# Two output projections cut into tiles of four contraction tiles by 512 columns, with the head norms moved behind their first tiles

## What is computed

```
mix1 = concat(gated linear attention heads (4 x 128), sliding window heads (8 x 64))   # 256 x 1024
o_gla = rms_norm(o_gla per head, gla_norm_w) * silu(gg)
x = x + gate * (mix1 @ attn_w_out)            # first block; then rms_norm and the first MLP
mix2 = concat(block attention heads (8 x 64), retention heads (4 x 128))               # 256 x 1024
ret = (ret - mean per head) * rsqrt(var per head + 1e-5) * ret_norm * silu(rg)
x = x + mix2 @ w_out_2                        # last block; then rmsnorm and the gated FFN
```

## Time and profile before

| | us |
|---|---|
| Median of 3 runs (1048.24 to 1051.0) | 1048.71 |
| Span of the profiled execution, first to last instruction | 1042.5 |
| TensorE busy | 935.5 (90%) |
| VectorE busy | 684.2 (66%) |
| ScalarE busy | 483.4 (46%) |
| GpSimd busy | 56.2 (5%) |
| HBM read | 194.38 MB, 187 GB/s over the span |
| Mean granted TensorE clock | 0.927 of full speed |

### The profile page before, as it was taken

One profiled execution on the slowest core, in us unless ns is written; L12 is line 12 of the kernel. 1 busy time (PEld: TensorE's weight loads), 2 busy tenths in 40 slices (PEclk: granted clock), 3 DMA queues, 4 the chain that ended last, 5 costly groups with the idle time before them and its releaser, 6 DMA issues.

```text
span 1042.5 us, 17856 instructions
## 1 busy us (share of the span) xinstructions
PE 935.5 (90%) x7128; PEld 893.5 (86%) x7128; DVE 684.2 (66%) x864; ACT 483.4 (46%) x566; POOL 56.2 (5%) x102
## 2 busy tenths in 40 slices
PE   1599987999999999599999996999876999999976
PEld 1398865989999999499999995988776999999976
DVE  5847977767887677665655457455546777666456
ACT  1426543346663325356663335444535565633353
POOL 2101111021111000000000000000000000000000
PEclk9689976979999997889999997999988999999988
DMA  9839764639988876047765554433413555655511
GB/s 327 282 132 313 265 200 141 201 101 320 324 309 298 273 250 222 0 142 228 236 218 164 193 174 137 160 123 124 160 41 106 178 175 187 208 162 176 192 41 41
DMA packets 156457, 196.09 MB, mean 188 GB/s; under 512 B 5325, under 2 KB 143100, under 8 KB 156412
## 3 DMA queue, kind: packets, MB, share of 16 engines
q1 hardware_dynamic: 142588, 145.12, 43.5%
q0 software_dynamic: 13824, 50.34, 13.2%
HBM read 194.38 MB, written 1.06 MB: 187 GB/s over the span
## 4 chain that ended last, share of the span: by engine, by line
PE 75%; DVE 14%; ACT 4%; issue 4%; DMA 1%; SPq 1%; DVEq 0%; ACTq 0%; POOLq 0%
PE G L517 15%; PE G L518 15%; PE G L519 15%; PE A L517 7%; PE A L518 7%; PE A L519 7%; DVE w_lo L949 2%; ACT w_hi L1537 2%; PE A L597 1%; PE A L577 1%; DVE HN L1096 1%; DVE ada_acc L967 1%; PE G L551 1%; PE G L552 1%; PE G L553 1%
## 5 line engine op out<-in xcount | busy, mean ns | idle before, releaser
L949 DVE TENSOR_TENSOR w_lo<-raw,w_hi 128x2048 fp32r<-128x2048 f32 (+1 forms) x135 | 307.1, 2275 | 228.8 <-ACT w_hi L1537 228.7
L517 PE MATMUL G<-h_hi,w_hi 128*128 128x256 f32 x1336 | 392.7, 294 | 44.4 <-DVE h_lo L1078 26.7
L1537 ACT ACTIVATE w_hi<-raw 128x2048 fp32r<-128x2048 f32 (+1 forms) x135 | 256.6, 1901 | 339.0 <-PE G L519 167.2
L518 PE MATMUL G<-h_lo,w_hi 128*128 128x256 f32 x1336 | 387.0, 290 | 0.0
L519 PE MATMUL G<-h_hi,w_lo 128*128 128x256 f32 x1336 | 386.5, 289 | 0.0
L517 PEld LDWEIGHTS G<-h_hi,w_hi 128*128 128x128 f32 x1336 | 265.6, 199 | 52.0 <-issue 38.4
L518 PEld LDWEIGHTS G<-h_lo,w_hi 128*128 128x128 f32 x1336 | 266.2, 199 | 0.5 <-issue 0.5
L519 PEld LDWEIGHTS G<-h_hi,w_lo 128*128 128x128 f32 x1336 | 265.7, 199 | 0.0
L517 PE MATMUL A<-u_hi,w_hi 128*128 128x256 f32 x512 | 143.6, 281 | 0.9 <-DVE X L1058 0.9
L518 PE MATMUL A<-u_lo,w_hi 128*128 128x256 f32 x512 | 143.2, 280 | 0.0
L519 PE MATMUL A<-u_hi,w_lo 128*128 128x256 f32 x512 | 143.2, 280 | 0.0
(11 more groups left out here) (265 smaller groups left out, 1058.6 us busy)
## 6 DMA issues: line engine op xcount, KB each, us to landing
raw<-in_mlp_w_dram SPq DMA_DIRECT2D x64, 1024.0 KB, 5.5
ada_raw<-in_ada_w_dram POOLq DMA_DIRECT2D x90, 512.0 KB, 5.3
raw<-in_w_in_dram SPq DMA_DIRECT2D x14, 1024.0 KB, 5.0
raw<-in_w_up_dram SPq DMA_DIRECT2D x11, 1024.0 KB, 5.3
raw<-in_w_gate_dram SPq DMA_DIRECT2D x11, 1024.0 KB, 5.3
raw<-in_attn_w_in_dram SPq DMA_DIRECT2D x9, 1024.0 KB, 12.2
raw<-in_w_down_dram SPq DMA_DIRECT2D x8, 1024.0 KB, 5.1
raw<-in_attn_w_out_dram SPq DMA_DIRECT2D x4, 1024.0 KB, 5.9
```

The source lines that it names most:

```text
L517: pe.matmul(dst, wh, ah, start=start, stop=False)
L518: pe.matmul(dst, wh, al, start=False, stop=False)
L949: dve.tensor_tensor(w_lo[n % 2][:, 0:k, :], raw[n % RAW][:, 0:k, :], w_hi[n % 2][:, 0:k, :].bitcast(F32), ALU.subtract).then_inc(lo_done, 1)
L1537: act.activation(w_hi[n % 2][:, 0:k, :], raw[n % RAW][:, 0:k, :], ACT.Copy).then_inc(hi_done, 1)
```

## The change

Both projections are cut another way: each of the four 1 MB blocks is now 4 tiles of the contraction by 512 columns. Blocks 0 and 1 are the attention half of the contraction for columns 0 to 511 and 512 to 1023; they open all four G banks and leave them open. Blocks 2 and 3 add the other half in the same banks. `out_block` does 48 matmuls, as a block did. In projection 1, block 0 stands ahead of the sums of squares; in projection 2, block 0 stands between means and variances and block 1 behind the variances. The retention scores of all four heads are made ahead of the last input block, in four banks. ScalarE makes the high half of block 11 (in projection 2: of blocks 93 and 94) ahead of the head roots, VectorE the low half likewise. On VectorE, projection 1's eleven pieces of modulation stood 4, 3, 2, 1, 1 and now stand 2, 2, 7; the seven come after the low halves of the normed activations and ahead of all four `residual_pair`. In projection 2 the gate product is moved behind the squares of the deviations. A residual may start when two of a block's four column tiles are done (`out_half`).

```diff
+OUT_TILES = ((slice(4, 8), slice(0, 4)), (slice(0, 4), slice(4, 8)))
...
+        def half_k(block):
+            return block[:, :, :].rearrange("p (a b) n -> p a (b n)", b=2)
...
-        take_each(*((f"rs{h}", h % 2) for h in range(4)))
-        take_each(("ro0", 2), ("ro1", 3), ("rm0", 0), ("rm1", 1), ("rv0", 2), ("rv1", 3), ("ms6", 2),
+        take_each(*((f"rs{h}", h) for h in range(4)))
+        take_each(("ro0", 0), ("ro1", 1), ("rm0", 2), ("rm1", 3), ("rv0", 0), ("rv1", 1), ("ms6", 2),
...
+            def load_half(n, w, tiles, half):
+                sp.wait_ge(lo_done, n - RAW + 1)
+                sp.dma_start(half_k(raw[n % RAW]), w[:, tiles, half * 2 * COLS:(half + 1) * 2 * COLS]
+                             ).then_inc(raw_full[n % RAW], 16)
...
+            def out_block(layer, j, split):
+                n, half, cut = (N_OUT, N_OUT2)[layer] + j, j // 2, j % 2
+                first = (U_OUT, U_OUT2)[layer] + 2 * cut
+                block_ready(n)
+                hi, lo = half_k(w_hi[n % 2]), half_k(w_lo[n % 2])
+                for m in range(4):
+                    u, cols = first + m // 2, slice(m * P, m * P + P)
+                    if half == 0 and m % 2 == 0:
+                        g_empty(u)
+                    for a in range(4):
+                        if cut == 0 and m == 0 and a % 2 == 0:
+                            pe.wait_ge(h_ready, 4 * SPLIT[split] + 2 * half + a // 2 + 1)
+                        ka = OUT_TILES[layer][half].start + a
+                        last = product(halves(G[u % 4])[:, m % 2, :], hi[:, a, cols], lo[:, a, cols],
+                                       h_hi[:, ka, :], h_lo[:, ka, :], half == 0 and m % 2 == 0 and a == 0,
+                                       half == 1 and a == 3, shared=True)
+                    if half == 1 and m == 1:
+                        last.then_inc(out_half, 1)
+                last.then_inc(block_used, 1)
...
+            out_block(0, 0, "mix0")
             for m in range(2):
                 pe.wait_ge(osq_ready, m + 1)
                 dst = bank_empty(pe, f"gm{m}")
...
-            for j in range(4):
-                feature_block(N_OUT + j, 9 + j, split="mix0" if j == 0 else None,
-                              order=(4, 5, 6, 7, 0, 1, 2, 3))
+            for j in range(1, 4):
+                out_block(0, j, "mix0")
...
-                    retention_scores((0, 1))
-            retention_scores((2, 3))
+                    retention_scores(range(4))
...
+                out_block(1, j, "mix1")
+            for j in (2, 3):
+                out_block(1, j, "mix1")
...
-            ada_next(1, 4)
             for a, p in enumerate((2, 3)):
                 low_pair("mix0", p, MIX[:, 2 * p:2 * p + 2, :], position=a)
+            ada_next(1, 2)
...
-            ada_next(1, 3)
+            ada_next(1, 2)
+            split_lo(N_OUT + 2)
...
-            for j in range(3):
-                split_lo(N_OUT + j + 2)
-                ada_next(1, (2, 1, 1)[j])
-                residual_pair(N_OUT + j, 9 + j, 2 * j, MOD[:, 0, 2 * DT:])
-            residual_pair(N_OUT + 3, 12, 6, MOD[:, 0, 2 * DT:])
+            split_lo(N_OUT + 3)
+            ada_next(1, 7)
+            for j in range(4):
+                residual_pair(N_OUT + 2 + j // 2, U_OUT + j, 2 * j, MOD[:, 0, 2 * DT:],
+                              half=0 if j % 2 else j // 2 + 1)
+                if j == 1:
+                    split_lo(N_OUT + 4)
...
+            split_lo(N_IN2 + 15)
+            split_lo(N_OUT2 + 2)
...
-            for j in range(3):
-                split_lo(N_OUT2 + j + 2)
-                residual_pair(N_OUT2 + j, U_OUT2 + j, 2 * j, None)
-            residual_pair(N_OUT2 + 3, U_OUT2 + 3, 6, None)
+            split_lo(N_OUT2 + 3)
+            for j in range(4):
+                residual_pair(N_OUT2 + 2 + j // 2, U_OUT2 + j, 2 * j, None, half=0 if j % 2 else 3 + j // 2)
+                if j == 1:
+                    split_lo(N_OUT2 + 4)
...
+            split_hi(N_OUT + 2)
             head_roots(("gm0", "gm1"), eps6)
...
             bank_was_read(act, "att_out17")
+            act.wait_ge(block_used, N_IN2 + 14)
             for p in range(2):
                 high_mix(p)
-            for m in range(2):
-                src = bank_full(act, f"ro{m}")
-                bank_read(f"ro{m}", act.activation(GG[:, 2 * m:2 * m + 2, :], halves(src), ACT.Copy))
+                src = bank_full(act, f"ro{p}")
+                bank_read(f"ro{p}", act.activation(GG[:, 2 * p:2 * p + 2, :], halves(src), ACT.Copy))
+            silu_parts(N_IN2 + 13, U_IN2 + 13, RT[:, 2:4, :], RG[:, 2:4, :])
+            split_hi(N_OUT2 + 1)
+            split_hi(N_OUT2 + 2)
             head_roots(("rv0", "rv1"), eps5)
```

More of the change, by code:

```diff
@@ L60 @@
 FDOWN_KT = (8, 8, 6)
-U_POOL, U_UP, U_IN2, U_OUT2, U_FFN, U_PLE, U_PLEG = 29, (13, 33), 49, 63, 67, 89, 93
+U_OUT, U_POOL, U_UP, U_IN2, U_OUT2, U_FFN, U_PLE, U_PLEG = 9, 29, (13, 33), 49, 63, 67, 89, 93
 C_ID, C_ANTI, C_HOT, C_MASK, C_DIST, C_DECAY, C_CNT = 0, 128, 256, 384, 512, 768, 1792
@@ L266, in build @@
         a_free = sems(*(f"a_free{n}" for n in range(4)))
-        down_half, down_free0, down_free1 = sems("down_half", "down_free0", "down_free1")
+        down_half, down_free0, down_free1, out_half = sems("down_half", "down_free0", "down_free1", "out_half")
         dve_step, act_step, pe_step = sems("dve_step", "act_step", "pe_step")
@@ L411, in _ @@
                 for j in range(4):
-                    load(N_OUT + j, w_out1[:, :, j * COLS:(j + 1) * COLS])
+                    load_half(N_OUT + j, w_out1, OUT_TILES[0][j // 2], j % 2)
                 for layer in range(2):
@@ L430, in _ @@
                 for j in range(4):
-                    load(N_OUT2 + j, w_out2[:, :, j * COLS:(j + 1) * COLS])
+                    load_half(N_OUT2 + j, w_out2, OUT_TILES[1][j // 2], j % 2)
                 with sp.Fori(0, 5) as i:
@@ L513, in _, with product @@
             chain = Chain(pe, pe_step)
[L515 to L519, removed]
+            def product(dst, wh, wl, ah, al, start, stop, shared=False):
+                pe.matmul(dst, wh, ah, start=start, stop=False, skip_group_check=shared)
+                pe.matmul(dst, wh, al, start=False, stop=False, skip_group_check=shared)
+                return pe.matmul(dst, wl, ah, start=False, stop=stop, skip_group_check=shared)
             def block_ready(n, i=0):
@@ L537, in feature_tile, with feature_block @@
                 return last
-            def feature_block(n, u, split=None, i=0, order=range(KT)):
+            def feature_block(n, u, split=None, i=0):
                 block_ready(n, i)
@@ L543, in feature_block @@
                     last = feature_tile(n, halves(G[u % 4])[:, m, :], slice(m * P, m * P + P),
-                                        [(k, k) for k in order], h_hi, h_lo, split=split if m == 0 else None)
+                                        [(k, k) for k in range(KT)], h_hi, h_lo, split=split if m == 0 else None)
+                last.then_inc(block_used, 1)
[17 more added lines that the diff above has]
+                        last.then_inc(out_half, 1)
                 last.then_inc(block_used, 1)
@@ L861, in _ @@
                     bank_done(f"ro{m}", last)
-            for name, src in (("rm", GG), ("rv", OSQ)):
+            for j, (name, src) in enumerate((("rm", GG), ("rv", OSQ))):
                 for m in range(2):
@@ L870, in _ @@
                                                       start=True, stop=True))
-            for j in range(4):
-                feature_block(N_OUT2 + j, U_OUT2 + j, split="mix1" if j == 0 else None)
+                out_block(1, j, "mix1")
+            for j in (2, 3):
+                out_block(1, j, "mix1")
             mean_square(6)
@@ L1024, in add_squares, with residual_pair @@
                 dve.wait_ge(ssq_ready, ssq[0])
-            def residual_pair(n, u, t, gate, squares=True):
-                dve.wait_ge(block_used, n + 1)
+            def residual_pair(n, u, t, gate, squares=True, half=0):
+                if half:
+                    dve.wait_ge(out_half, half)
+                else:
+                    dve.wait_ge(block_used, n + 1)
                 src = halves(G[u % 4])
@@ L1403, in _ @@
             for h in range(4):
-                if h == 2:
-                    split_lo(N_IN2 + 15)
                 src = bank_full(dve, f"rs{h}")
@@ L1424, in _ @@
                 dve.tensor_tensor(OSQ[:, 2 * m:2 * m + 2, :], o, o, ALU.mult).then_inc(osq_ready, 1)
+            for m in range(2):
+                u = U_IN2 + 12 + m
+                dve.wait_ge(g_free[u % 4], u // 4 + 1)
+                chain(dve.tensor_tensor(RG[:, 2 * m:2 * m + 2, :], RG[:, 2 * m:2 * m + 2, :],
+                                        RT[:, 2 * m:2 * m + 2, :], ALU.mult))
+            split_lo(N_IN2 + 15)
+            split_lo(N_OUT2 + 2)
             for m in range(2):
@@ L1750, in _ @@
```

(5 more changed lines are left out.)

## The result

Twelve runs of each kernel: the changed one takes 1052.2 us (1047.82 to 1057.27), the one before 1048.53 (1045.65 to 1051.58). The ratio of the two is 1.0038, with a 95% interval of 1.0019 to 1.0056: 4.0 us slower, 2.0 to 5.9 (the medians alone lie 3.7 apart). The forecast was 1050.1 in a range of 1044 to 1055, most likely "same", with 0.29 on slower by over 0.3%; it came out just past that line.

A forecast was written before the change was run, and what follows sets the result against it. TensorE was taken to bound the kernel, with VectorE setting projection 1's end. +8.4 and -7.0 gave +1.4 us on the 1042.5 us span, 1043.9; 6.2 more for the median gave 1050.1, range 1044 to 1055.

The forecast's parts named there:

- its two terms: Span change split by projection: projection 1 ends 8.4 us later, projection 2 ends 7.0 us sooner.
- the slow rival: Projection 2, clock falls in the gap ahead of block 2, costing 2.2 us: +3.6, 1052.3 in all; chance 0.25.
- what would show it wrong: No wait for `ada_raw`, a residual ahead of the pieces, clock 0.5 in block 2, or head roots before block 0's end.
- 2.0 said: Projection 2: TensorE waits 2.0 us at the fourth head's score until VectorE copies the last attention output.
- 18 said: Projection 1: TensorE idle from block 3 to the mean square for 18 us.
- The loads of the blocks, put at nothing: Loads of the new 1 MB blocks cost nothing, covered by ScalarE's wait for TensorE of up to 6.20 us.
- +8.4 said: Projection 1: last residual's end moves from 208.0 to 216.4, 8.4 us later, behind seven modulation pieces with three buffers.
- 22.5: Projection 1, ScalarE: the head norm's exponentials start at 181.8, 6.3 us later than before.
- the median for both: Projection 1: both reloads VectorE waits for land 5.1 us after issue, the median of eleven; least 3.7, most 6.9.
- -7.0 said: Projection 2: residuals end at 784.9 against 791.9, 7.0 us sooner, with no modulation in the queue.
- the open price: Projection 2, clock across the new gap ahead of block 2: nothing lost assumed; 1.5 to 2.2 us if it falls.
- 3.0 said: Projection 2: TensorE idles 3.0 us ahead of block 2, waiting for the normed half.

The follow-up runs named there:

- combo2: Changed kernel with modulation pieces standing 3, 3, 2, 1, 2, logarithm table load earlier, last attention copy earlier: 1034.13 us, ratio 0.9854.
- combo3: Changed kernel with modulation pieces standing 3, 4, 1, 1, 2, logarithm table load earlier, last attention copy earlier: 1033.77 us, ratio 0.9869.
- after: The changed kernel itself, both projections in the new order, against the kernel before the change: 1052.2 us, ratio 1.0038.
- p1_only: Changed kernel with projection 2 taken back to its old form on all engines: 1055.59 us, ratio 1.0055.
- att_first: Changed kernel with VectorE copying the last attention output ahead of the low half before it: 1050.52 us, ratio 1.0006.
- ada_late: Changed kernel with the seven modulation pieces spread 3, 2, 1, 1 among the residuals: 1052.92 us, ratio 1.0034.
- ada_241_4: Changed kernel with modulation pieces standing 2, 4, 1, 4 in place of 2, 2, 7: 1045.55 us, ratio 0.9968.
- ada_33212: Changed kernel with modulation pieces standing 3, 3, 2, 1, 2 in place of 2, 2, 7: 1038.0 us, ratio 0.9895.
- preload: Changed kernel with ScalarE's logarithm table load moved ahead of a high half in both projections: 1047.01 us, ratio 0.998.

## Why the prediction was right

**In short.** The time fell in the range, and the order of work was as drawn up, but the sum was not what happened. It had a change of +1.4 us and 4.0 was measured; of its two terms one was 2.0 too high and the other 3.9 too low, so that in part they made up for each other, which is luck. Measured, 1052.2, is the slow rival's time (1052.3), and what it turned on, the clock in block 2 of projection 2, came about; a granted clock of 0.5 in block 2 was on the prediction's own list of what would show it wrong.

**Mechanism.** The order of events was there: block 0 behind the attention outputs, three pieces, a wait, three pieces, a wait, one, four residuals; TensorE done sooner and waiting; a wait of 1.83 us at the fourth score (2.0 said); a gap ahead of block 2 in both. TensorE stood 15.8 us from its last block to the mean square, the sums of the modulation's columns within them (18 said). The loads of the blocks, put at nothing, cost nothing that the trace shows: ScalarE's high halves still waited for TensorE (5.88 and 5.97 us in its rows). The Trainium skill's estimate of 3.2 us for a 512 KB transfer like those of `ada_raw` (DMA: Bandwidth & Descriptors, "Anatomy of one DMA — SWDGE (gpsimd) path") was again not met: the shortest in projection 1 took 3.7 in the changed kernel and 3.6 in any kernel here (`combo2`, `combo3`).

**Projection 1: +8.4 said, +6.4 measured.** Two terms were too large. The exponentials start at 184.33, 21.5 behind the copy, where I had 22.5 (181.8 - 159.34): TensorE's clock rose sooner in block 0 (6 matmuls came at the slow pace, where I had 16). And the waits were 5.6 us, not 6.6: the last transfer took 3.7, the least, and I had put the median for both. Block 2 lost its clock here (188.86 to 196.42 is 7.6 us in place of 5.8), which cost nothing, VectorE being behind.

**Projection 2: -7.0 said, -3.1 measured** (-3.7 up to the last square). The step that failed is the open price: "I take nothing lost, by the nearest row". Ahead of block 2 TensorE waited 3.46 us (3.0 said), and the clock fell, as the slow rival had it. TensorE's windows after:

```profile
784.00:786.00 2.00, 1.48 (x7) 1.51 (x8) 1.04 (x2) 2.00 (x2) 0.00 (x0) 0.51 0.00 0
786.00:788.00 2.00, 2.00 (x13) 2.00 (x13) 1.85 (x1) 0.11 (x1) 0.00 (x0) 0.64 0.00 0
```

Block 2 took 784.52 to 791.89, 7.4 us, so 1.6 lost. I had not thought of the second place: the 1.83 us wait ahead of the fourth score was followed by a slow last input block too, 755.9 to 763.2, 1.5 lost. In four of the other five kernels with that wait the same block ran at full clock, so what brought the clock down there is not shown. Another 0.5 went at the norm, where the mean square ran slow. 7.0 less 3.6 is 3.4, near the 3.1 measured. The rival's price for one such place (2.2) was above the 1.6 measured, and its count of places too low.

**Sum.** +1.4 said, +3.2 in the stretches, 4.0 by the runs. I also added 6.2 us for what lies around the span. That is 1.7 (1054.21 for a span of 1052.5); the other 4.5 was a quick execution of the kernel before, quicker by that reckoning (1044.2) than any that was timed (1045.25 the least). This has no effect on the difference, only on how far a single span can be trusted: not to 5 us.

## What to carry to other kernels

Time freed on the busiest engine is only gained if the engine that takes its results can follow: here TensorE came out 4.5 us sooner and the stretch ended 6.4 later, because seven loads-and-adds with three buffers had been put in front of the residuals. When filler work moves, price each piece by when its buffer is free and its reload in, and give the last one its own due time, by who needs the sum. Put it where the new order makes the engine idle: that turned a loss of 0.4% into a gain of 1%.

## What was not expected of the hardware

The length of TensorE's gap did not settle whether the clock fell. Ahead of block 2 of projection 1, gaps of 3.20 and 3.21 us: in `after`, `p1_only` and `att_first` the clock fell in the block, in `ada_late`, `ada_241_4` and `ada_33212` it did not, with the same instructions on TensorE. Gaps of 1.56 (`preload`) and 1.87 (`combo3`) kept it there and one of 3.07 (`combo2`) lost it. One that kept it:

```profile
186.59 0.36 PE L529 MATMUL G<-h_hi,w_hi 128*128 128x256 f32 x1 [3.20 <-DVE h_lo L1116]
...
186.00:188.00 2.00, 1.41 (x12) 1.44 (x13) 1.11 (x2) 2.00 (x2) 0.00 (x0) 1.00 0.56 228
188.00:190.00 2.00, 2.00 (x19) 2.00 (x18) 1.78 (x1) 0.19 (x1) 0.00 (x0) 1.00 0.00 0
```

In projection 2, 3.46 us (3.47 in one) lost it in five kernels of six, and 1.83 us in all three that had it (`preload`, `combo2`, `combo3`). The 1.83 us ahead of the fourth score were followed by a slow last input block in two kernels of six (after, `ada_241_4`). 12 to 26 matmuls came at 0.21 us each time, 1.1 to 2.4 us. So no rule of length is to be had from these traces, and a gap of 2 to 3.5 us at such a place should be priced, as an estimate from these rows, between nothing and 2.4 us. What decides it stays open; it would take many profiles of one kernel.
